# Two chunks in flight in the last cross-attention, and x chunks behind the products of the first SSD

## The reference, cut to what matters

```
xn = RMSNorm(h);  [z | xBC | dt | q | k | v] = xn @ w_in
mix = concat(SSD(z, xBC, dt), window_attention(q, k, v)) @ w_out
h = h + mix
h = h + CrossAttn(RMSNorm(h), memory K/V)      # 4 heads of 128 over 256 memory tokens
h = h + SwiGLU(RMSNorm(h));  y = RMSNorm(h)
```

## Time and profile before

| | |
|---|---|
| median of 3 runs | 3036.34 us (3033.49 to 3038.89) |
| the profiled execution | 3037.64 us, of which the span is 3035.6 |
| TensorE matmuls busy | 2847.7 us, 94% of the span |
| VectorE, ScalarE, GpSimd busy | 48%, 38%, 33% |
| mean granted TensorE clock | 0.963 of 2.4 GHz |
| first SSD, 386 to 483 us: TensorE busy, clock | 59.3 of 97.0 us, 0.75 |
| last cross-attention, 2494 to 2543.5 us: the same | 24.7 of 49.5 us, 0.72 |

### The profile page before, as it was taken

One profiled execution on the slowest core, in us unless ns is written; L12 is line 12 of the kernel. 1 busy time (PEld: TensorE's weight loads), 2 busy tenths in 40 slices (PEclk: granted clock), 3 DMA queues, 4 the chain that ended last, 5 costly groups with the idle time before them and its releaser, 6 DMA issues. The chain is left out here.

```text
span 3035.6 us, 34742 instructions
## 1 busy us (share of the span) xinstructions
PE 2847.7 (94%) x13537; PEld 2281.6 (75%) x13537; DVE 1462.8 (48%) x2216; ACT 1165.4 (38%) x1875; POOL 1003.3 (33%) x451
## 2 busy tenths in 40 slices
PE   7858968999999999999999999999999986999998
PEld 3436856787877878878778887878778765888886
DVE  3244556555765246556663265557652434222224
ACT  2234544444344224543453244543442233322222
POOL 1112202333333433343234434333334431333331
PEclk9879978999999999999999999999999997999998
DMA  9352356422222335322223354222223340222221
GB/s 312 113 144 63 118 143 156 107 81 87 70 76 77 97 104 160 90 84 80 70 73 94 97 161 110 78 82 72 74 78 97 111 143 28 77 80 81 84 78 63
DMA packets 415093, 303.03 MB, mean 100 GB/s; under 512 B 48075, under 2 KB 384079, under 8 KB 413890
## 3 DMA queue, kind: packets, MB, share of 16 engines
q1 hardware_dynamic: 412474, 294.41, 32.8%
q10 hardware_dynamic: 1880, 6.34, 0.6%
q0 software_dynamic: 576, 0.07, 0.0%
HBM read 277.90 MB, written 23.85 MB: 99 GB/s over the span
## 5 line engine op out<-in xcount | busy, mean ns | idle before, releaser
L1528 POOL TENSOR_TENSOR w_lo<-w_raw,w_hi 128x1024 fp32r<-128x1024 f32 x400 | 975.2, 2441 | 1831.4 <-ACT w_hi L1542 1831.4
L1542 ACT ACTIVATE w_hi<-w_raw 128x1024 fp32r<-128x1024 f32 x400 | 421.3, 1054 | 545.7 <-PE G L2730 270.5
L2453 PE MATMUL L<-xa_h,w_hi 128*128 128x512 f32 x1184 | 476.5, 402 | 0.0
L2454 PE MATMUL L<-xa_h,w_lo 128*128 128x512 f32 x1184 | 465.1, 393 | 0.0
L2455 PE MATMUL L<-xa_l,w_hi 128*128 128x512 f32 x1184 | 465.1, 393 | 0.0
L2453 PEld LDWEIGHTS L<-xa_h,w_hi 128*128 128x128 f32 x1184 | 225.0, 190 | 54.5 <-issue 6.7
L2455 PEld LDWEIGHTS L<-xa_l,w_hi 128*128 128x128 f32 x1184 | 224.4, 190 | 48.4
L2454 PEld LDWEIGHTS L<-xa_h,w_lo 128*128 128x128 f32 x1184 | 225.1, 190 | 46.1 <-issue 1.0
L2453 PE MATMUL L<-xb_h,w_hi 128*128 128x512 f32 x576 | 231.4, 402 | 10.3 <-DVE xb_l L1919 10.3
L2455 PE MATMUL L<-xb_l,w_hi 128*128 128x512 f32 x576 | 225.5, 391 | 0.0
L2454 PE MATMUL L<-xb_h,w_lo 128*128 128x512 f32 x576 | 225.5, 391 | 0.0
(11 more groups left out here) (532 smaller groups left out, 5031.0 us busy)
## 6 DMA issues: line engine op xcount, KB each, us to landing
w_raw<-in_w_down_dram SPq DMA_DIRECT2D x88, 512.0 KB, 3.4
w_raw<-in_w_gate_dram SPq DMA_DIRECT2D x66, 512.0 KB, 3.8
w_raw<-in_w_up_dram SPq DMA_DIRECT2D x66, 512.0 KB, 3.8
w_raw<-in_w_in_dram SPq DMA_DIRECT2D x56, 512.0 KB, 3.8
xt<-xT_dram SPq DMA_DIRECT2D x56, 256.0 KB, 4.2
w_raw<-in_w_gate_dram SPq DMA_DIRECT2D x44, 256.0 KB, 2.8
w_raw<-in_w_up_dram SPq DMA_DIRECT2D x44, 256.0 KB, 3.1
fwin<-in_w_in_dram SPq DMA_DIRECT2D x8, 1156.0 KB, 10.1
```

The source lines that it names most:

```text
L1528: pool.tensor_tensor(w_lo[:, n % RING, 0:w], w_raw[:, n % RING, 0:w], w_hi[:, n % RING, 0:w].bitcast(F32), ALU.subtract)\
L1542: act.activation(w_hi[:, n % RING, 0:w], w_raw[:, n % RING, 0:w], ACT.Copy)\
L2453: pe.matmul(acc, wh, rh, start=(k == 0), stop=False)
L2454: pe.matmul(acc, wl, rh, start=False, stop=False)
```

## The change

Four things are changed.

1. The twelve x chunks get another place in the first SSD. For TensorE, chunks 4 to 7 come in beats 0 to 3, and the others in pairs behind the last products of each SSD chunk (beats 6, 9, 12, 15); for ScalarE the pairs come behind the exponentials (beats 5, 8, 11) and, the last, behind the squares of the last chunk. SyncE issues the load of chunk c+2 ahead of the store of chunk c, where it was c+1.
2. 1/rms of the twelve chunks is computed once at the end instead of three times, and the three `r_out` stores go out together behind all x chunks. `load_rb(1)` waits for all three.
3. In all SSDs VectorE makes the next decay factors behind the gated output instead of ahead of it.
4. The cross-attention of block 3 is a function of its own, `last_cross`, on each engine. Scores of odd chunks go to the two banks of `L`, so scores and exponentials of two chunks are in flight. Its keys and values are loaded by ScalarE's queue at the fifth W panel of block 3, into other space (`km3_h`, `km3_l`, `vm3`, where the high part of the input projections' operand was).

```diff
+km3_h = at("km3_h", O_B, [P, CH, NMEM], F32R)
+km3_l = at("km3_l", O_B + 4096, [P, CH, NMEM], F32R)
+vm3 = at("vm3", O_B + 8192, [P, 2, CH * P])
...
-    sp.wait_ge(s["rx_ready"], g)
+    sp.wait_ge(s["rx_ready"], 1)
...
-def r_group(dve, g):
-    dve.wait_ge(s["x_sq"], 4 * g + 4)
-    cols = slice(4 * g, 4 * g + 4)
+def r_group(dve, g, end):
+    dve.wait_ge(s["x_sq"], 4 * end)
+    cols, w = slice(4 * g, 4 * end), 4 * (end - g)
-    rsqrt(dve, rx[:, 2, cols], rx[:, 1, cols], small[:, 7, 0:4])
+    rsqrt(dve, rx[:, 2, cols], rx[:, 1, cols], small[:, 7, 0:w])
...
-SSD_BEATS = 19
-CHUNK_AT = {beat: C + i for i, beat in enumerate((0, 1, 2, 4, 5, 7, 8, 10, 11, 13, 14, 16))}
+PE_CHUNKS = {0: [4], 1: [5], 2: [6], 3: [7], 6: [8, 9], 9: [10, 11], 12: [12, 13], 15: [14, 15]}
+ACT_CHUNKS = {0: [4], 1: [5], 2: [6], 3: [7], 5: [8, 9], 8: [10, 11], 11: [12, 13], 15: [14, 15]}
...
+    def last_scores(c, h):
+        return (G if c % 2 == 0 else L)[:, h // 2, (h % 2) * 256:(h % 2) * 256 + 256]
...
-            sp.wait_ge(s["r_out"], 16 * b)
+            sp.wait_ge(s["r_out"], 16 * (NBLK - 1))
...
                 if b == 0 and n == w0 + 4:
                     sp.wait_ge(s["piece"], piece_index[("V", CH - 1)] + 1)
                     x_chunk_in(sp, C)
+                    x_chunk_in(sp, C + 1)
                     for c in range(C, 4 * NBLK):
-                        if c + 1 < 4 * NBLK:
-                            x_chunk_in(sp, c + 1)
+                        if c + 2 < 4 * NBLK:
+                            x_chunk_in(sp, c + 2)
                         x_chunk_out(sp, c)
-                        if c % 4 == 3:
-                            r_out(sp, c // 4)
+                    for g in range(1, NBLK):
+                        r_out(sp, g)
                     sp.wait_ge(s["x_out0"], 16 * (2 * NBLK - 2))
                     sp.wait_ge(s["x_out1"], 16 * (2 * NBLK - 2))
                     load_rb(1)
...
+        def memory_in(high, low, values_):
+            act.dma_start(high[:].bitcast(F32), kmh_dram.ap().rearrange("p (h m) -> p h m", h=CH)).then_inc(s["km_in"], 16)
+            act.dma_start(low[:].bitcast(F32), kml_dram.ap().rearrange("p (h m) -> p h m", h=CH)).then_inc(s["km_in"], 16)
+            act.dma_start(values_[:], vm_dram.ap().rearrange("p (c n) -> p c n", c=2)).then_inc(s["km_in"], 16)
+        def last_cross():
+            w0 = C * (NBLK - 1)
+            def exps(c):
+                act.wait_ge(s["xmax"], w0 + c + 1)
+                if c >= 2:
+                    act.wait_ge(s["xpt"], w0 + c - 1)
+                for h in range(CH):
+                    act.activation(PC[:, c % 2, h, :], last_scores(c, h), ACT.Exp, bias=cs_[:, c % 2, 0, h:h + 1],
+                                   accum_out=cs_[:, c % 2, 1, h:h + 1]).then_inc(s["xexp"], 1)
+            exps(0)
+            exps(1)
+            for c in range(C):
+                act.wait_ge(s["xpt"], w0 + c + 1)
+                act.wait_ge(s["xo"], w0 + c - 1)
+                act.activation(PTc[:, c % 2], G[:, 2:4, :].rearrange("p a (i t) -> p (a i) t", t=P), ACT.Copy)\
+                   .then_inc(s["xptsb"], 1)
+                if c + 2 < C:
+                    exps(c + 2)
+                act.wait_ge(s["xo"], w0 + c + 1)
+                act.activation(cq_h[:, :, c * P:c * P + P], bank(4).rearrange("p (h t) -> p h t", t=P),
+                               ACT.Copy).then_inc(s["o_hi"], 1)
...
-            if beat in CHUNK_AT:
-                x_chunk_act(act, CHUNK_AT[beat])
+            for c in ACT_CHUNKS.get(beat, []):
+                x_chunk_act(act, c)
...
+                if not more and n == 4:
+                    act.wait_ge(s["lin_out"], out_of("W", b, 0) + 1)
+                    memory_in(km3_h, km3_l, vm3)
...
-            act.wait_ge(s["lin_out"], out_of("Q", b, CH - 1) + 1)
-            act.dma_start(km_h[:].bitcast(F32), kmh_dram.ap().rearrange("p (h m) -> p h m", h=CH)).then_inc(s["km_in"], 16)
-            act.dma_start(km_l[:].bitcast(F32), kml_dram.ap().rearrange("p (h m) -> p h m", h=CH)).then_inc(s["km_in"], 16)
-            act.dma_start(vm[:], vm_dram.ap().rearrange("p (c n) -> p c n", c=2)).then_inc(s["km_in"], 16)
-            over = cross(b)
+                act.wait_ge(s["lin_out"], out_of("Q", b, CH - 1) + 1)
+                memory_in(km_h, km_l, vm)
+                over = cross(b)
-            for _ in over:
-                pass
+                for _ in over:
+                    pass
+            else:
+                last_cross()
...
                 dve.tensor_tensor(state[:], state[:], bank(5), ALU.add)
                 yield
                 dve.wait_ge(s["yd"], cc + 1)
-                if c + 1 < C:
-                    decay_factor(c + 1)
                 dve.drain()
                 dve.tensor_tensor(yac[:], yac[:], bank(0), ALU.add)
                 dve.drain()
                 dve.tensor_tensor(zs[:, :, c * P:c * P + P], yac[:].rearrange("p (i n) -> p i n", n=P),
                                   bank(1).rearrange("p (i n) -> p i n", n=P), ALU.mult).then_inc(s["y_done"], 1)
+                if c + 1 < C:
+                    decay_factor(c + 1)
                 yield
             dve.wait_ge(s["ysq"], 8 * (b + 1))
             dve.tensor_scalar(ssg[:, 1, :], ssg[:, 0, :], 1.0 / 256, EPS, ALU.mult, ALU.add)
...
+        def last_cross():
+            w0 = C * (NBLK - 1)
+            def maxima(c):
+                dve.wait_ge(s["xs"], w0 + c + 1)
+                src = G[:, 0:2, :] if c % 2 == 0 else L[:, 0:2, :]
+                dve.tensor_reduce(cs_[:, c % 2, 0, :], src.rearrange("p a (h m) -> p (a h) m", h=2),
+                                  AX_X, ALU.max, negate=True).then_inc(s["xmax"], 1)
+            def shares(c):
+                dve.wait_ge(s["xexp"], CH * (w0 + c + 1))
+                dve.reciprocal(cs_[:, c % 2, 2, :], cs_[:, c % 2, 1, :])
+                dve.drain()
+                dve.tensor_tensor(PC[:, c % 2], PC[:, c % 2],
+                                  cs_[:, c % 2, 2, :].unsqueeze(2).to_broadcast([P, CH, NMEM]), ALU.mult)\
+                   .then_inc(s["xprob"], 1)
+            maxima(0)
+            maxima(1)
+            shares(0)
+            shares(1)
+            for c in range(C):
+                if c + 2 < C:
+                    maxima(c + 2)
+                dve.wait_ge(s["o_hi"], w0 + c + 1)
+                cols = slice(c * P, c * P + P)
+                dve.tensor_tensor(cq_l[:, :, cols], bank(4).rearrange("p (h t) -> p h t", t=P),
+                                  cq_h[:, :, cols].bitcast(F32), ALU.subtract).then_inc(s["o_lo"], 1)
+                if c + 2 < C:
+                    shares(c + 2)
...
-            if CHUNK_AT.get(beat, 0) % 4 == 3:
-                r_group(dve, CHUNK_AT[beat] // 4)
+            if beat == 16:
+                r_group(dve, 1, NBLK)
...
+        def last_cross():
+            w0 = C * (NBLK - 1)
+            def scores(c):
+                if c >= 2:
+                    pe.wait_ge(s["xexp"], CH * (w0 + c - 1))
+                for h in range(CH):
+                    o = last_scores(c, h)
+                    qh, ql = cq_h[:, h, c * P:c * P + P], cq_l[:, h, c * P:c * P + P]
+                    pe.matmul(o, qh, km3_h[:, h, :], start=True, stop=False)
+                    pe.matmul(o, qh, km3_l[:, h, :], start=False, stop=False)
+                    last = pe.matmul(o, ql, km3_h[:, h, :], start=False, stop=True)
+                last.then_inc(s["xs"], 1)
+            pe.wait_ge(s["cq_lo"], CH * NBLK)
+            pe.wait_ge(s["km_in"], 48 * NBLK)
+            scores(0)
+            scores(1)
+            for c in range(C):
+                pe.wait_ge(s["xprob"], w0 + c + 1)
+                pe.wait_ge(s["xptsb"], w0 + c)
+                for i in range(2 * CH):
+                    last = pe.transpose(G[:, 2 + i // 4, (i % 4) * P:(i % 4) * P + P],
+                                        PC[:, c % 2, i // 2, (i % 2) * P:(i % 2) * P + P], ident[:])
+                last.then_inc(s["xpt"], 1)
+                if c + 2 < C:
+                    scores(c + 2)
+                pe.wait_ge(s["xptsb"], w0 + c + 1)
+                if c >= 1:
+                    pe.wait_ge(s["o_lo"], w0 + c)
+                for h in range(CH):
+                    for m in range(2):
+                        last = pe.matmul(bank(4)[:, h * P:h * P + P], vm3[:, m, h * P:h * P + P],
+                                         PTc[:, c % 2, 2 * h + m, :], start=(m == 0), stop=(m == 1))
+                last.then_inc(s["xo"], 1)
...
-            if beat in CHUNK_AT:
-                x_chunk_pe(pe, CHUNK_AT[beat])
+            for c in PE_CHUNKS.get(beat, []):
+                x_chunk_pe(pe, c)
```

More of the change, by code:

```diff
@@ L2280, in _ @@
                     x_chunk_dve(dve, c)
-                r_group(dve, 0)
+                r_group(dve, 0, 1)
                 diagonal(rx[:, 1, 0:C])
```

## The result

The changed kernel takes **3000.47 us** (median of 4 runs, 2997.65 to 3001.78), against 3036.39 us for the kernel before on the same chip (4 runs, 3033.49 to 3038.89). The ratio is 0.9882, 95% interval 0.9869 to 0.9894: some 36 us less. The forecast was 3019, 17 less; its rival (a), in which the r stores overlap, said 3003.

A forecast was written before the change was run, and what follows sets the result against it. TensorE, busy 94% of the span, was taken to bound the kernel. Terms -21 + 16.8 + 1.5 - 15 = -17.7 against the profiled 3037.64 gave 3019.9, or 3019 as median; range 3000 to 3029.

The forecast's parts named there:

- rival (a): Behind the first SSD: the three r stores overlap, +2.5 instead of +18.3, total 3003 us; chance 0.25.
- part 2: r stores bunched behind the first SSD: SyncE holds later loads until all land, +16.8 us, plus +1.5 for the clock.
- the serial value: r stores behind the first SSD write one after another, 3 + 3 x 7.6 = 25.8 us; x tile +16.8 us.
- Split of a store: One r store's 10.6 us to land, taken as some 3 of latency and 7.6 of writing.
- T: Issue time of the last r store before, and of all three after, behind the first SSD's x chunks.
- The clock's +1.5: Block 0's W: TensorE drops to 1.2 GHz in the pause, first matmuls behind it at half speed, +1.5 us.
- Part 1: First SSD: x chunks placed behind the products, 11.6 us a chunk instead of 16.3; -21 us, bounds -12 to -27.
- the lead-in: Start of the first SSD: four chunks ahead of the first product instead of three, loads begun earlier; -1 us (0 to -2).
- rival (b): First SSD: x chunks still bind it, gain there only -8 us, total 3032 us; chance 0.1.
- Part 3: Last cross-attention: early key and value loads -6.9 us, two chunks in flight -8.1; -15 in all, bounds -8.5 and -19.9.
- Costed at nothing: ScalarE's three loads in the last W stage, and later decay factors in blocks 1 to 3, both at 0.
- Rival (c): r stores behind the first SSD hinder each other, slower from 16 us of writing each; at 17, 3046 us; chance 0.05.

The follow-up runs named there:

- e2: The changed kernel with r again computed for four chunks at a time in the first SSD, each r store behind its fourth x chunk; 3004.77 us, ratio 0.9891.
- e6: The changed kernel with six more r stores, to scratch nobody reads, behind the three, and the wait for all nine; 3010.86 us, ratio 0.9929.
- e7: The changed kernel with the x chunks back at their old beats; 3007.1 us, ratio 0.9915.
- e5: The changed kernel with VectorE's decay factors ahead of the gated output again; 3002.6 us, ratio 0.99.
- e1: The kernel before with only r computed once and its three stores issued together behind the last x chunk, all waited for; 3029.48 us, ratio 0.9984.
- e9: The kernel before, r computed at its old places, only the three r stores moved behind the last x chunk and waited for together; 3030.26 us, ratio 0.9992.

## Why the prediction was wrong

The forecast was 3019 and the kernel takes 3000.47: the change gives 36 us where 17 were expected. The step that failed is the choice in part 2, "I take the serial value": +16.8 for stores that write one after another, 7.6 us each, and +1.5 for the pause behind them. Measured, three stores hold the queue 11.2 us, about as long as one, and W as a whole takes 0.5 us more. Step by step:

- **Split of a store, "some 3 of latency and 7.6 of writing": wrong.** Three stores held SyncE's queue 11.2 us, against 25.8 forecast and "about T + 11.5" in rival (a). From three to nine stores each adds 2.4 us on average; from one to three, next to nothing. The first x tile came 3.0 us later (forecast +16.8; the lower bound was +2.5).
- **The evidence for it was misread.** "The loads behind a store crawl as if its engines were occupied": the crawl is there (an x load of 14.4 us in e2, 15.1 in before), and by the traces nearly all of such a load is held until the store has landed. That says nothing of how long a second *store* takes. And it means that in before the x tiles were already held for the whole of one store, landing 2.8 us behind it; a wait for three that take no longer than one could then cost only little. I had one case of a load behind a store, and none of a store behind a store, and carried the one over to the other. What holds the load is not settled; it is not the order within one queue, since with the store in another queue four x loads still took 11.2 to 12.1 us.
- **The Trainium skill's two rules on it** (DMA: Bandwidth & Descriptors, Specifications and Bandwidth). The read-modify-write below 512 B gives no duration, and no run here shows what share it has in these times. At the floor of about 10.5 ns a packet, which that page of the Trainium skill measured on loads issued from GpSimd, 1536 packets would be 16 us behind the latency and the 4608 elements of nine stores 48 us, an estimate from its figure; the stores were through in 11.2 and 25.7 us with all latency. The measurement decides: that floor does not hold for these elements on this kernel's queues.
- **The clock's +1.5 behind the pause**: the pause did not come, nor did the 1.5. Behind the 15.6 us pause of e6 the clock is down: the matmuls there take 0.63 us instead of 0.39.
- **W of block 0 as a whole, +18.3 forecast: +0.5 by these two profiles.** The wait for `xb_l` at the k projection was 3.3 us before and 1.4 after and varied between none and 3.4 among the profiles; against e2, with the same 1.4, the late tiles cost 4.0. Either is far from 18.3.
- **Part 1, -21: measured -22.8, but in part for a reason I had costed at zero.** The three chunk steps give -16.8 (forecast -14.1), chunk 3 up to the end of its products -6.8 (-5.8), the lead-in +0.3 (-1; at an equal clock -1.3) and what follows +0.5 (0). "The last r computation ... 0" is true of the last, but I never priced the two that disappear and the two stores that no longer stand in front of x loads. With the r part undone (e2) the SSD gives only -13.0 (95.65 to 82.70; -14.6 at an equal clock), towards the weak end of my bounds (-12); the r part brings the other 9.8. The forecast of 11.6 us a chunk has no r computation in it, while the 16.3 before had, so the gain of moving r stood in my -14.1 without a name (measured 10.5 to 11.2, with the clock up; my bound was 10.4).
- **Inside part 1** the chunk beats bring 9.3 (e7) and the decay factors 2.8 (e5), or 4.4 at an equal clock. x loads waited for: 0.4, so rival (b) is out.
- **Part 3, -15: measured -17.0.** Early loads 9.1 where I had 6.9: up to the first score they give 7.1, close to it. The other 2.0 I left out: TensorE comes out of that 9 us wait at 1.2 GHz, and the first scores group now takes 1.7 us instead of 2.9. That is 1.2 of the 2.0; the rest I can't show. Two in flight 8.0 where I had 8.1.
- **Costed at nothing and right:** the loads by ScalarE in the W stage, and the decay factors in blocks 1 to 3, as far as the scatter lets one see.
- **Rival (a)** gave 3003, near the measured time, and had the stores right: the queue free at T + 11.2 (it said 11.5), the tile at T + 17.06 (16.5). That the total fits as well is partly luck, since the r part as a whole is not +2.5 but a gain, about -5 by e1's ratio (-1 to -8), part of which stood in my -21. Rival (c), 16 us of writing for each store, is out: all three together took 11.2.

Together: -22.8 for the SSD, +0.5 for W, -17.0 for the cross-attention, +3.6 in the stretches that the change doesn't touch, which is their scatter: -35.7, as between the spans.

## What to carry to other kernels

When a transfer is grouped with others of its kind, a single one's time from issue to landing says nothing of what two more cost: look for, or make, a case with the number that you need. Do not carry a slope past the counts at which it was measured; here one to three stores cost about the same and nine did not. When a load lands late, see what it stood behind: here it was held already, so that one more wait ahead of it cost little. When work is moved out of a chain, credit the place that it leaves before debiting the place where it goes: here the small computation and the small stores were worth 10 us where they stood and cost 4 where they went (after against e2). And where a late datum passes through memory only to be spread over partitions, a product with ones under cover of a projection can take it off the queue altogether.

## What the runs showed of the hardware

- Stores of 512 separate 4-byte elements: single ones landed in 9.0 to 11.0 us with x transfers beside them, three in one queue were through 10.3 to 11.6 us after the first issue (11.2 in after), nine after 25.7 (one profile).
- A 512 KB load issued behind such a store is held, but for a trickle, until the store has landed: the queues moved 22 GB/s while one was out and 257 after it (e2), and the loads landed in up to 14.4 (e2) and 15.1 us (before), where without a store the twelve took at most 5.7 (after) and 6.2 (e9). This also holds with the store in another engine's queue (11.2 to 12.1, four loads in one profile).
- TensorE's clock in the first SSD stayed up when its pauses went: a granted 1.00 where it had been 0.81, and the heads of three chunks took 0.60 us instead of 1.11 for the same four transposes. The mean granted clock over the span is 0.969 in the profile after, against 0.963 before.
